# A planned order of TensorE's work gets least distances between steps, waits by token tile, and small products in the opening

## Time and profile before

| what | value |
|---|---|
| timed runs, median (lowest to highest) | 1026.44 us (1026.02 to 1027.26) |
| profiled execution, own time | 1035.11 us |
| its span | 1033.3 us |
| TensorE busy, weight loads busy | 985.7 us, 825.9 us |
| DVE, ACT, POOL busy | 450.4, 391.7, 391.2 us |
| mean granted TensorE clock | 0.984 |

### The profile page before, as it was taken

How to read it: one execution, slowest core, us unless ns; L and a number is a source line. 1 busy time by engine, 2 the same in 40 slices (tenths; PEclk the granted TensorE clock), 3 DMA queues, 4 the chain that set the end, 5 groups by cost and what they waited for, 6 DMA issues and landing times.

```text
span 1033.3 us, 13229 instructions
## 1 busy us (share of the span) xinstructions
PE 985.7 (95%) x5059; PEld 825.9 (80%) x5059; DVE 450.4 (44%) x954; ACT 391.7 (38%) x727; POOL 391.2 (38%) x302
## 2 busy tenths in 40 slices
PE   7998989999999999889999889899999999999997
PEld 5886878778788888888888877787888888888886
DVE  4573652398545346175459635561001100222224
ACT  3433333356553253125463633443222222233332
POOL 4570432355215342012123014454443544444441
PEclk9999999999999999689999999999999999999999
DMA  6272221411243241141211111215323233232222
GB/s 212 67 219 46 88 92 41 133 42 62 79 165 121 82 144 31 33 152 42 82 42 62 42 31 52 75 49 177 99 85 119 82 98 105 82 118 86 85 79 82
DMA packets 70815, 92.54 MB, mean 90 GB/s; under 512 B 11469, under 2 KB 49906, under 8 KB 70754
## 3 DMA queue, kind: packets, MB, share of 16 engines
q1 hardware_dynamic: 70754, 91.71, 27.9%
HBM read 89.57 MB, written 6.85 MB: 93 GB/s over the span
## 4 chain that ended last, share of the span: by engine, by line
PE 83%; DVE 8%; issue 3%; ACT 2%; DMA 2%; POOL 1%; SPq 0%; DVEq 0%; POOLq 0%; ACTq 0%
PE psum L1180 62%; PE psum L1441 5%; PE psum L1401 3%; PE psum L1416 3%; PE psum L1493 2%; PE psum L1367 1%; PE psum L1265 1%; PE psum L1469 1%; PE psum L1454 1%; DMA RAW<-in_w_gate_up_dram 1%; DVE XT L1935 1%; DMA r_scratch<-st 1%; DVE R L1906 1%; PE psum L1226 1%; PE psum L1483 1%
## 5 line engine op out<-in xcount | busy, mean ns | idle before, releaser
L2323 POOL TENSOR_TENSOR WR<-RAW,WR 128x512 fp32r<-128x512 f32 (+3 forms) x268 | 354.7, 1336 | 583.4 <-ACT WR L1583 583.0
L1180 PE MATMUL psum<-WR,XT 128*128 128x512 f32 (+3 forms) x2160 | 532.3, 393 | 9.4 <-DVE XT L1935 3.4
L1180 PEld LDWEIGHTS psum<-WR,XT 128*128 128x128 f32 x2160 | 389.5, 191 | 79.2 <-issue 9.3
L1583 ACT ACTIVATE WR<-RAW 128x512 fp32r<-128x512 f32 (+3 forms) x268 | 159.5, 614 | 248.1 <-PE psum L1180 238.0
L1180 PE MATMUL psum<-XT,WR 128*128 128x512 f32 x1056 | 240.8, 390 | 3.7 <-POOL WR L2323 1.9
L1180 PEld LDWEIGHTS psum<-XT,WR 128*128 128x128 f32 x1056 | 197.8, 188 | 45.3 <-POOL WR L2323 2.4
L1718 ACT ACTIVATE prob<-prob,st 128x512 f32<-128x512 f32 (+2 forms) x112 | 58.9, 547 | 117.9 <-DVE st L2104 107.2
L1948 DVE TENSOR_TENSOR gated<-psum,r_bc 128x512 f32<-128x512 f32 x22 | 14.2, 686 | 176.0 <-PE psum L1180 161.6
L1441 PEld LDWEIGHTS psum<-ones_up,probT 128*128 128x128 f32 x536 | 71.9, 193 | 7.0 <-issue 1.2
L1441 PE MATMUL psum<-ones_up,probT 128*128 128x128 f32 x536 | 73.8, 277 | 0.4 <-ACT ones_up L881 0.2
L2293 DVE TENSOR_TENSOR XT<-actT,XT 128x512 fp32r<-128x512 f32 x22 | 28.3, 1285 | 83.6 <-ACT XT L1775 83.6
(11 more groups left out here) (231 smaller groups left out, 820.1 us busy)
## 6 DMA issues: line engine op xcount, KB each, us to landing
RAW<-in_w_gate_up_dram SPq DMA_DIRECT2D x44, 512.0 KB, 4.8
RAW<-in_w_in_dram SPq DMA_DIRECT2D x13, 1024.0 KB, 5.2
RAW<-in_w_down_dram SPq DMA_DIRECT2D x11, 1024.0 KB, 4.8
RAW<-in_w_out_dram SPq DMA_DIRECT2D x8, 1024.0 KB, 5.1
RAW<-in_w_in_dram SPq DMA_DIRECT2D x14, 512.0 KB, 4.9
rep_scratch<-rows_scratch SPq DMA_DIRECT2D x12, 320.0 KB, 6.6
RAW<-in_w_in_dram SPq DMA_DIRECT2D x4, 768.0 KB, 4.3
R<-in_x_dram SPq DMA_DIRECT2D x8, 256.0 KB, 6.0
```

Of the source, the lines that this page charges most:

```text
L1180: last = pe.matmul(outp, stationary(x), moving(y), start=start and n == 0, stop=stop and n == 2)
L1583: act.activation(WR[:, s % RING, 0, 0:w], RAW[:, g % 2, q, 0:w], ACT.Copy).then_inc(w_hi, 1)
L2323: pool.tensor_tensor(WR[:, s % RING, 1, 0:w], RAW[:, g % 2, q, 0:w], WR[:, s % RING, 0, 0:w].bitcast(F32), ALU.subtract).then_inc(w_lo, 1)
```

## The change

It has six parts.

1. **Least distances.** `flush` keeps in `given` the position at which each step was put into the list, and `ready` holds a step back until q is at least that of its predecessor plus a lag from a new table: 26 pairs of kinds (LAGGED) with a number each (PLAN["lags"]). Score after q/k transposes 2, transpose after score 2, output after transpose 2, CS_b after CS 4, CO after CS_b 3, CT after CS 2, CO after CT 1, Z after qt 9, F after sp_b 3 and so on; 12 of the 26 are zero.
2. **Positions.** Many starts and lags of PLAN change with it; the fox group starts at 83 instead of 76, moba at 130 instead of 123 with its norm's last transposes at 147 instead of 133.
3. **Waits by token tile.** The first product of a half of XT waits for its own tile's xt (not in gu); the first xt steps of out1 and out2 wait for their own tile's evacuation; `rest` lets a product in once its own tile's xt is in the list.
4. **Compression.** "hidden" becomes four steps of 32 matmuls, each with its gelu, at 64, 65, 67 and 68 instead of two steps at 64 and 67.
5. **Bias sums.** "windows" goes two parts at a time after k = 0, 1, 2, and "cmp_bias" after k = 3 instead of 5.
6. **Opening.** Products of ones, 128 x 128 x 128 in float32, whose result nobody reads, 3, 4, 3, 0, 3 and 6 of them at six places; the second half of the gain row after the second xt; the splits between the xt steps; `setup` moved from before ("qa", "fox", 0) to ("zero", "moba"), right after chunk 0.

```diff
+SPINS = (3, 4, 3, 0, 3, 6)
+LAGGED = {("S", "qt"): 0, ("T", "S"): 1, ("O", "T"): 2, ("qt", "qb"): 3, ("F", "sp_b"): 4, ("OS", "F"): 5, ("CS", "cmpkv"): 6,
+          ("CT", "CS"): 7, ("CO", "CT"): 8, ("gm", "gm_b"): 9, ("xt", "gx"): 10, ("T", "O"): 11, ("cmpkv", "hidden"): 12,
+          ("hidden", "blocks"): 13, ("blocks", "qt"): 14, ("Z", "qt"): 15, ("qb", "qa"): 16, ("CO", "CS_b"): 17, ("CS_b", "CS"): 18,
+          ("sp_b", "sp"): 19, ("sp", "Z"): 20, ("S", "T"): 21, ("Z", "F"): 22, ("qt", "ev"): 23, ("gates1", "ev"): 24, ("gelu", "ev"): 25}
-PLAN = {'norm_fox': (41, 12, 5, 7), 'logf': 65, 'C': (76, 3), 'fox': (76, 8, 3, 6, 9), 'norm_moba': (101, 5, 3, 14), 'moba': (123, 9, 3, 4, 9), 'qt_sb': (164, 2), 'sb': (174, 11, 2, 8, 13, 18, 3, 28), 'norm_swa': (196, 6, 4, 11), 'swa': (231, 6, 2, 5, 9), 'gates1': (234, 260), 'gx_out1': (238, -5), 'xt_out1': (255, -1), 'out1': (66,), 'qt_cmp': (35, 4), 'gates2': 38, 'blocks': 55, 'hidden': (64, 67), 'cmpkv': 70, 'qt_q': (63, 2), 'qt_slc': (66, 3), 'qt_win': (105, 3), 'cmp': (74, 3, 3, 4, 6), 'slc': (88, 6, 2, 6, 9), 'win': (136, 6, 2, 6, 9), 'gelu': (135, 158), 'gm_a': (137, 4), 'gm_b': (144, 4), 'gm_w': (142, 12), 'gm': (161, 6), 'xt_out2': (170, 4), 'out2': (46, 44, 49, 47)}
+PLAN = {'lags': (2, 2, 2, 0, 3, 2, 0, 2, 1, 0, 2, 0, 0, 0, 0, 9, 0, 3, 4, 1, 0, 0, 3, 0, 1, 0), 'norm_fox': (42, 11, 7, 5), 'logf': 66, 'C': (84, 2), 'fox': (83, 8, 3, 7, 10), 'norm_moba': (105, 8, 3, 15), 'moba': (130, 7, -2, 4, 10), 'qt_sb': (163, 2), 'sb': (174, 11, 3, 8, 13, 18, 3, 27), 'norm_swa': (196, 6, 4, 11), 'swa': (231, 5, 2, 4, 10), 'gates1': (234, 260), 'gx_out1': (238, -13), 'xt_out1': (256, -1), 'out1': (66,), 'qt_cmp': (35, 4), 'gates2': 38, 'blocks': 55, 'hidden': (64, 65, 67, 68), 'cmpkv': 69, 'qt_q': (63, 2), 'qt_slc': (67, 4), 'qt_win': (105, 3), 'cmp': (74, 3, 3, 5, 6), 'slc': (88, 6, 2, 6, 10), 'win': (136, 6, 2, 6, 10), 'gelu': (135, 158), 'gm_a': (138, 4), 'gm_b': (145, 4), 'gm_w': (144, 12), 'gm': (162, 6), 'xt_out2': (170, 1), 'out2': (46, 43, 51, 47)}
...
     def flush(q, product=None):
 
+        def ready(step):
+            for other in follows(step):
+                if other not in given:
+                    return False
+                pair = (step[0], other[0])
+                if pair in LAGGED and q < given[other] + PLAN["lags"][LAGGED[pair]]:
+                    return False
+            return True
+
         held.extend(sorted(before.pop(q, []), key=order))
-        done = set(tl)
         moved = True
         while moved:
             moved = False
             for step in list(held):
-                if done.issuperset(follows(step)):
+                if ready(step):
                     held.remove(step)
                     tl.append(step)
-                    done.add(step)
+                    given[step] = q
                     moved = True
         if product:
             quarter(*product, q % NT)
             if q % NT == NT - 1 and product[2] == KD - 1:
                 tl.append(("ev", *product[:2]))
+                given[tl[-1]] = q + 1
...
-        first_row = ("xt", phase, 3, halves(phase)[0])
         while before or held or products:
             flush(q)
-            if products and products[0][0] <= q and first_row in tl:
-                n = products.pop(0)[1]
-                quarter(phase, 0, n, sum(x[0] in ("mm", "mq") and x[1:4] == (phase, 0, n) for x in tl))
+            if products and products[0][0] <= q:
+                n = products[0][1]
+                t = sum(x[0] in ("mm", "mq") and x[1:4] == (phase, 0, n) for x in tl)
+                if ("xt", phase, t, halves(phase)[0]) in given:
+                    products.pop(0)
+                    quarter(phase, 0, n, t)
...
-    tl.extend([("zero", "fox"), ("gain_row",)])
+    tl.extend([("zero", "fox"), ("spin", 0), ("gain_row", 0), ("spin", 1)])
     tl.append(("gx", "in1", 0, 0))
     for t in range(NT):
         if t + 1 < NT:
             tl.append(("gx", "in1", t + 1, 0))
         tl.append(("xt", "in1", t, 0))
-    for s in range(4):
-        tl.append(("split", s))
+        if t == 1:
+            tl.append(("gain_row", 1))
+        tl.append(("spin", 2 + t))
+        if t:
+            tl.extend(("split", s) for s in {1: (0,), 2: (1,), 3: (2, 3)}[t])
...
-    on(PLAN["hidden"][0], ("hidden", 0))
-    on(PLAN["hidden"][1], ("hidden", 1))
+    for n in range(4):
+        on(PLAN["hidden"][n], ("hidden", n // 2, n % 2))
...
-            if c == 0 and k < 6:
-                tl.append(("windows", k))
-                if k == 5:
-                    tl.append(("cmp_bias",))
+            if c == 0 and k < 3:
+                tl.extend([("windows", 2 * k), ("windows", 2 * k + 1)])
+            if c == 0 and k == 3:
+                tl.append(("cmp_bias",))
...
+            def wait_tile_evacuated(prev, t):
+
+                who = evac_engine(prev[1], prev[2], t)
+                done = ev_count[prev][0 if who == "act" else 1]
+                mine = [u for u in range(NT) if evac_engine(prev[1], prev[2], u) == who]
+                pe.wait_ge(ev_act if who == "act" else ev_dve, done - len(mine) + mine.index(t) + 1)
...
+                if what == "spin":
                     pe.wait_ge(setup_dve, 1)
+                    for _ in range(SPINS[step[1]]):
+                        pe.matmul(XB[3][:, 0:P], ones_up[:, 0:1].broadcast_to([P, P]), ones_up[:, 0:1].broadcast_to([P, P]),
+                                  start=True, stop=True)
+                elif what == "gain_row":
+                    hf = step[1]
                     pe.wait_ge(s_gain, 16)
-                    for hf in range(2):
-                        pe.matmul(XB[hf], ones_up[0:1, 0:1].broadcast_to([1, P]), gain_row[0:1, 512 * hf:512 * hf + 512],
-                                  start=True, stop=True).then_inc(gain_rows, 1)
+                    pe.matmul(XB[hf], ones_up[0:1, 0:1].broadcast_to([1, P]), gain_row[0:1, 512 * hf:512 * hf + 512],
+                              start=True, stop=True).then_inc(gain_rows, 1)
...
-                        elif (phase, hf) == ("out1", 0):
-                            wait_evacuated(pe, ("ev", "in1", 7))
-                            wait_evacuated(pe, ("ev", "in2", 4))
-
+                    if (phase, hf) == ("out1", 0):
+                        wait_tile_evacuated(("ev", "in1", 7), t)
+                    elif (phase, hf) == ("out2", 1):
+                        wait_tile_evacuated(("ev", "in2", 4), t)
...
-                    if ch == 0 and n % 4 == 0 and what == "mm":
+                    if ch == 0 and n % 4 == 0 and phase == "gu":
...
+                        if ch == 0 and n % 4 == 0 and phase != "gu":
+                            pe.wait_ge(xt_lo, nth["xt", phase, t, halves(phase)[n // 4]] + 1)
...
-                    for f in range(2):
-                        for m in range(16):
-                            last = pe.matmul(SC[nth[step] % 2][:, 64 * f:64 * f + 64], w1[kv][:, m, P * f:P * f + P],
-                                             blocks[:, kv, m, :], start=m == 0, stop=m == 15)
+                    for m in range(16):
+                        last = pe.matmul(SC[nth[step] % 2][:, 0:64], w1[kv][:, m, P * f:P * f + P],
+                                         blocks[:, kv, m, :], start=m == 0, stop=m == 15)
...
-                if step == ("qa", "fox", 0):
+                if step == ("zero", "moba"):
```

More of the change, by code:

```diff
@@ L197, in follows @@
         else:
-            out.append({"sb": ("ev", "in1", 4), "cmp": ("ev", "in2", 0), "q": ("ev", "in2", 1), "slc": ("hidden", 1), "win": ("ev", "in2", 2)}[name])
+            out.append({"sb": ("ev", "in1", 4), "cmp": ("ev", "in2", 0), "q": ("ev", "in2", 1), "slc": ("hidden", 1, 1), "win": ("ev", "in2", 2)}[name])
         return out + {"sb": [("S", "fox", 3, 2)], "swa": [("S", "moba", 3, 2)]}.get(name, [])
@@ L280, in make_timeline @@
     }
-    before, held = {}, []
+    before, held, given = {}, [], {}
     def order(step):
@@ L1486, in _ @@
                 elif what == "hidden":
-                    kv = step[1]
+                    _, kv, f = step
                     wait_sc(step)
@@ L1584, in _ @@
                 elif what == "gain_row":
-                    for hf in range(2):
-                        act.wait_ge(gain_rows, hf + 1)
-                        act.activation(gain[0][:, 512 * hf:512 * hf + 512], XB[hf], ACT.Copy).then_inc(gain_copied, 1)
+                    hf = step[1]
+                    act.wait_ge(gain_rows, hf + 1)
+                    act.activation(gain[0][:, 512 * hf:512 * hf + 512], XB[hf], ACT.Copy).then_inc(gain_copied, 1)
                 elif what == "xt":
```

38 lines of the change are left out of this document (17 added, 21 removed).

## The result

| kernel | times, median (lowest to highest) | ratio to before, 95% interval |
|---|---|---|
| before, beside it | 1026.33 us (1026.02 to 1027.26, 4 runs) | |
| changed | 1012.18 us (1010.65 to 1015.24, 4 runs) | 0.9864 (0.984 to 0.9889) |
| changed, once more | 1009.98 us (1008.58 to 1010.54, 6 runs) | 0.9806 (0.976 to 0.9853) |

The change makes the kernel faster by 14.2 us, not by the 25.4 forecast; 1012.2 lies in the range of 990 to 1014, at its upper end. The two ratios are those of means, and beside "once more" the kernel before had 4 of its 11 runs at 1034 to 1038; against the other seven (median 1025.6) the ratio there is 0.985. All ten runs of the changed kernel have a median of 1010.5, and experiments are compared with that. The profiled execution took 1015.24 (span 1013.4), a second one 1009.97 (span 1008.2), so it spans 19.9 and 25.1 us less than the profiled one of before.

The account below looks back on a forecast made before the run. TensorE's own work, its waits and its slow clock were taken as the bound. Ten terms summed to 27.4 us; 1026.4 - 27.4 = 999.0, or 1011.8 without the clock loss; forecast 1001, range 990 to 1014.

Parts of the forecast that it names:

- The signs given in advance: Would-be evidence in the profile: among others, first weight product at about 12, TensorE's waits at least 12 us smaller in sum.
- Term 1: Opening: earlier splits start the first weight product sooner, products of ones raise the clock; 4.6 us (1.3 to 5.0).
- Rival (c): Opening: the products of ones don't lift the clock; 3.3 us less gain, 1004; no chance given.
- Term 2: Norms and setup: moving setup worth nothing, first transposes one quarter later; 0.3 us (-0.5 to 1.8).
- Terms 3 and 4: Start of fox (2.2 us) and moba (0.7): later positions and lags cover TensorE's waits, less new piles in moba.
- Rival (e): Positions put the waits elsewhere and all but terms 1 and 6 come back: 1020 to 1026; chance 0.07.
- Term 5: End of in1: out1's first transposes wait per tile instead of for all four evacuations; 1.2 us (0 to 1.6).
- Term 6: Windows and bias sums: earlier sums use DVE's idle time, removing TensorE's wait of 1.77; 1.8 us (0 to 2.0).
- Term 7 and 8: Compression: a wait goes and the clock stays up, 11.4 us; cmp branch: lags shorten CO's waits for probT, 1.3.
- Rival (a): Compression: the clock falls all the same, for the narrow matmuls; 16.3 us less, 1010; chance 0.20.
- Term 9 and 10: Out2: waits per tile remove two waits and a slow-clock stretch, 4.4 us; added xt steps and later outputs, -0.5.
- Rival (b): DVE becomes the bound in moba and cmp, terms 3, 4 and 8 come to nothing: 1008; chance 0.12.

Follow-up runs that it names:

- experiment 2: The changed kernel with the old position table and zero distances (plan_before, 1019.21 us), or only the compression's old pairs of halves (hidden_pairs, 1011.3 to 1022.1).
- experiment 5: The changed kernel with TensorE's waits for evacuations and xt rows over all four tiles, as before: 1017.5 us.
- experiment 3: The changed kernel with paired halves of hidden but no wait ahead (1013.5 to 1015.9 us), or halves apart with a wait made (median 1021.45).
- pairs_no_wait: The changed kernel with hidden's halves paired again and qt of q and slc in steps of four quarters: 1013.5 to 1015.9 us.
- hidden_pairs: The changed kernel with hidden's halves paired, cmpkv and qt of slc as before: three runs at 1011.3 to 1012.3 us, three at 1018.5 to 1022.1.
- plan_before: The changed kernel with the position table of before and all least distances 0: median 1019.21 us.

## Why the prediction was right or wrong

**The step that failed** is the one behind the sum: "The forecast is 1001, near the first, as three runs within 1.2 us look like one and the same course". They were one course, but not that of the profile. The prediction had the other number too: 1011.8, if they lack the loss to the clock. Three equal runs 8.7 us below the profiled one pointed to that. By the runs, two of three executions of before never lose what experiment 2 puts at 9.3 us, and a median can't win it. 27.4 - 9.3 = 18.1 would have given 1008.3; measured are 1010.5 over all ten runs. The range held because its upper part was made for this case. That the result came so near the 1011.8 is luck in part: in the second profile out2 gives 4.7 us more than was said, sb and the windows 4.3 and 3.5 less.

The signs given in advance: TensorE's waits add up to some 41 us before and 26 in the first profile after, 15 less where at least 12 were asked; the first product at about 12 came in the other profiles only (12.6 to 14.0).

- **Term 1 (4.6)**: 3.8 in the second profile, -0.6 in the first. The steps were right: with the splits 2.4, with an early rise of the clock 0.4 to 1.7 more; first product at 12.6 to 14.0 (predicted 12.1) in nine of ten profiles, clock up at 7.6 to 10.3 (predicted 6.5 to 7). Its lower end of 1.3 was too high, since the sum for the slow case, 15.4, has 1.8 for the xt steps, and they take 3.6 at that pace: the product started at 17.2. Rival (c) is that one execution in ten.
- **Term 2 (0.3)**: 0.4.
- **Terms 3 and 4 (2.9)**: 3.4; the wait for "issue" is gone, the piles of moba cost less than assumed.
- **No term for sb**: the greatest miss of the early part, 4.3 us. I looked at the entries that had changed by much and took Z's step from 2 to 3 for nothing. With the larger step TensorE waited for DVE's parts, and 3.5 came back when it was 2 again (and the last output one quarter later). Rival (e) named the mechanism, without a place.
- **Term 5 (1.2)**: 2.5, or 2.1 with out1's start, of which 1.9 is the wait by tile (experiment 5).
- **Term 6 (1.8)**: 3.2 in the runs. The wait went as said, and a short fall with it; two parts at a time cost the clock 1.7 to 5 us again, which "55 small matmuls stay 55" left out.
- **Term 7 and 8 (12.7)**: 12.9 and 13.0 against the profiled execution. The mechanism was right, the wait brings the fall (experiment 3), but that the sum fits is luck: the clock was worth 9.3 and not 11.1, the waits 3.6 and not 1.6. Rival (a), the narrow matmuls alone, is refuted for 64 columns: no long fall in 16 runs of pairs_no_wait and of the changed kernel. The waits were set too low: the wait for cmpkv that I took for sure did not come, and kS_slc's got shorter.
- **Term 9 and 10 (3.9)**: 8.6. The second half gave 3.4 as said (1.7 and 1.7). The other 5.2 came earlier: the wait of 1.04 ahead of the first product is gone as said, the 2.47 that the term left as it was became 1.80, one of 1.68 for DVE ahead of the first transposes of out2 became 1.22, and the clock's short fall at 579.7 of before (1.7) did not come again in any of the twelve profiles with the new waits or positions. That fall was no term; the rest, 1.3, I can't name.
- **Start of gu, no term**: up to 4.1 given back. The wait for POOL there is 3.1 us in the first profile and 2.1 in the second (1.9 before); the clock fell twice there in the first and not in the second, on the same list. Yet it is not chance alone. In 11 of the 12 profiles of the changed kernel and its variants the clock falls somewhere in gu, in one of the two of before; the first 200 matmuls of gu take 49.9 to 53.6 us in the twelve (mean 52.1), 49.8 and 51.0 in the two. So the forecast left out some 1.7 us, and why the clock falls there more often no run shows.
- **Rival (b)**: not seen; CO's 2.0 us of waits for DVE are 0.5.

## What to carry to other kernels

Before a loss in the profiled execution goes into a forecast of the median, ask whether the timed runs have it: a gap between the two is itself a row, and a loss to the clock can be there in one execution of three. A wait of 1.7 to 2.8 us right ahead of a run of narrow matmuls can cost several times its length, in some executions or in all; take the wait away rather than reshape the matmuls, and spread very narrow ones evenly between wide ones. In a table of positions a step of one quarter more can cost as much as the largest wait that the table removes, and positions tuned with least distances are worth less than nothing without them (1040.6, against 1010.5 with them and 1025.9 before).

## What the runs showed of the hardware

- One and the same list gives two times some 10 us apart on one core, by whether TensorE's clock falls once: 56 and 28 of 84 runs of the kernel before.
- The clock fell with no wait in TensorE's timeline, where 20 matmuls of 16 columns stand between 408-column ones (ten of ten profiles), and did not there with 10 of them in a row (four profiles).
- With a wait of 2.78 us ahead of narrow matmuls 12 of 12 runs were slow, by a median of 10.9 us; with one of 1.74, 8 of 18 (hidden_pairs and plan_before). Waits of 2.25 and 3.55 us with mostly wider matmuls after them brought no fall and one of 3.4 us (pairs_no_wait, one profile).
- The clock stayed at half through 12 us of matmuls of 64 columns in a row, without a wait between them (hidden_pairs).
- TensorE without a gap from 1.13 us on got its full clock at 7.6 us in one execution and at 17.5 in another.
